# Hybrid attention and MoE layer on one core: softmax sums applied to the turned result of a head pair, attention steps in groups of two units

## What is computed

```python
h  = rms_norm(x, g_attn)
z  = h @ w_in                        # q, k, v of branch a (MoBA) and b (DSA), indexer, two gates
# branch a: causal attention; branch b: attention over the 128 keys that the indexer picks
s_own = einsum('bqhd,bhkd->bqhk', q_c, k_own) * scale        # causal mask, then
p_own = softmax(s_own, axis=-1)
o     = einsum('bqhk,bhkd->bqhd', p_own, v_own)              # softmax(scores) @ V per head
x = x + (sigmoid(ga) * (o_a @ w_br_a) + sigmoid(gb) * (o_b @ w_br_b)) @ w_out
x = x + hier_moe(rms_norm(x, g_ffn), ...)                    # 32 experts, two per token
x = x + sigmoid(rms_norm(x, g_ple) @ w_ple_gate) * (p @ w_ple_proj)
```

## Time and profile before

| | us |
|---|---|
| runs: 999.1, 998.84, 1000.87; median | 999.1 |
| profiled execution, whole | 998.48 |
| its span (first to last instruction) | 996.7 |
| busy in the span: TensorE | 967.7 (97%) |
| TensorE weight loads | 593.6 (60%) |
| VectorE | 380.4 (38%) |
| ScalarE | 305.9 (31%) |
| GpSimd | 134.7 (14%) |
| mean granted clock of TensorE | 0.997 |

### The profile page before, as it was taken

One profiled execution on the slowest core, in us unless ns is written; L12 is line 12 of the kernel. 1 busy time (PEld: TensorE's weight loads), 2 busy tenths in 40 slices (PEclk: granted clock), 3 DMA queues, 4 the chain that ended last, 5 costly groups with the idle time before them and its releaser, 6 DMA issues.

```text
span 996.7 us, 12099 instructions
## 1 busy us (share of the span) xinstructions
PE 967.7 (97%) x4818; PEld 593.6 (60%) x4818; DVE 380.4 (38%) x785; ACT 305.9 (31%) x536; POOL 134.7 (14%) x137
## 2 busy tenths in 40 slices
PE   8999999999999999999999999999998998999996
PEld 6776887676788888886434444444443443443475
DVE  4344896655353536327211111110111111013776
ACT  6445335746433214242111111111111111211555
POOL 0320234926500000000000100000000000001000
PEclk9999999999999999999999999999999999999998
DMA  9512230000082350856999999999999999999902
GB/s 333 183 49 79 85 92 2 2 1 2 1 296 85 94 195 7 350 201 249 414 391 423 419 421 421 422 421 420 421 420 420 421 420 422 415 421 405 369 1 85
DMA packets 59145, 256.05 MB, mean 257 GB/s; under 512 B 12222, under 2 KB 12862, under 8 KB 34000
## 3 DMA queue, kind: packets, MB, share of 16 engines
q1 hardware_dynamic: 50224, 248.26, 62.4%
q0 software_dynamic: 2560, 4.20, 1.1%
q10 hardware_dynamic: 6304, 2.80, 1.1%
HBM read 248.95 MB, written 10.49 MB: 260 GB/s over the span
## 4 chain that ended last, share of the span: by engine, by line
PE 81%; DMA 12%; DVE 2%; POOL 2%; ACT 2%; issue 0%; DVEq 0%; SPq 0%
PE psum L749 37%; PE psum L1119 17%; DMA slot<-in_w_up 12%; PE psum L1075 5%; PE psum L1139 4%; PE psum L1140 4%; PE psum L1095 1%; PE psum L1159 1%; PE psum L1261 1%; PE psum L1085 1%; PE psum L964 1%; PE psum L949 1%; PE psum L937 1%; POOL raw L2211 1%; PE psum L737 1%; PE psum L925 1%
## 5 line engine op out<-in xcount | busy, mean ns | idle before, releaser
L1119 PE MATMUL psum<-slot,xt 128*64 128x512 f32 x512 | 232.7, 598 | 10.1 <-DMA slot<-in_w_up 9.4
L1120 PE MATMUL psum<-slot,xt 128*64 128x512 f32 x512 | 232.9, 598 | 0.0
L1119 PEld LDWEIGHTS psum<-slot,xt 128*64 128x64 f32 x512 | 65.8, 137 | 131.9 <-issue 127.7
L1139 PE MATMUL psum<-slot,ht 128*64 128x512 f32 x256 | 115.9, 595 | 0.0
L1140 PE MATMUL psum<-slot,ht 128*64 128x512 f32 x256 | 115.9, 596 | 0.0
L749 PE MATMUL psum<-w_hi,act_hi 128*128 128x512 f32 x288 | 114.8, 399 | 0.3 <-DVE act_lo L1655 0.3
L2227 POOL DMA_INDIRECT pair_rows<-y,slot_pair x30 | 30.3, 1012 | 618.3 <-ACT y L1500 618.3
L749 PE MATMUL psum<-w_lo,act_hi 128*128 128x512 f32 x288 | 112.5, 391 | 0.0
L749 PE MATMUL psum<-w_hi,act_lo 128*128 128x512 f32 x288 | 112.3, 390 | 0.0
L574 DVE TENSOR_TENSOR w_lo<-raw,w_hi 128x2048 fp32r<-128x2048 f32 (+1 forms) x30 | 69.3, 2308 | 90.3 <-ACT w_hi L569 90.2
L1493 ACT ACTIVATE small<-psum,slot_inv 64x512 f32<-64x512 f32 x32 | 21.9, 684 | 250.3 <-PE psum L1120 249.3
(11 more groups left out here) (294 smaller groups left out, 1490.1 us busy)
## 6 DMA issues: line engine op xcount, KB each, us to landing
slot<-in_w_gate SPq DMA_DIRECT2D x64, 1024.0 KB, 21.2
slot<-in_w_up SPq DMA_DIRECT2D x64, 1024.0 KB, 20.7
slot<-in_w_down SPq DMA_DIRECT2D x64, 1024.0 KB, 22.0
raw<-in_w_in SPq DMA_DIRECT2D x21, 1024.0 KB, 5.1
raw<-in_w_out SPq DMA_DIRECT2D x4, 1024.0 KB, 5.7
pair_in<-pair_rows SPq DMA_DIRECT2D x4, 1024.0 KB, 14.8
slot<-in_w_ple_gate SPq DMA_DIRECT2D x4, 1024.0 KB, 12.3
rows_tok<-in_x SPq DMA_DIRECT2D x8, 256.0 KB, 5.2
```

The lines of the kernel that those rows point to most:

```text
L1119: mm_g = pe.matmul(ps[FIRST:2 * FIRST, :], left, g[:, k, :], start=first, stop=last)
L1120: mm_u = pe.matmul(ps[0:FIRST, :], left, u[:, k, :], start=first, stop=last)
L1139: pe.matmul(ps[0:FIRST, :], left, w[:, k, 0:512], start=first, stop=last)
```

## The change

Four things change together:

- P is no longer scaled. Its turn on TensorE waits for ScalarE's exponential (`exps_to` counts them in their new order) instead of GpSimd's scaling.
- GpSimd spreads the two inverted sums of a unit over 64 columns each (`spread_sums`) into `sums_wide`. A new step `turn_s` per head pair transposes these four blocks on TensorE into bank 5. ScalarE copies the bank into `ot_sum`, which also gives the bank back. VectorE multiplies the pair's result bank by it into `ot_sum`. GpSimd then makes the high and the low part (`split_rows`), in place of ScalarE and VectorE.
- The attention steps go in groups: scores of two units, turn of one, pv of two, turn of the next, and behind every second group `turn_s`. VectorE inverts sums for two units at a time, and ScalarE waits for the spread four units back before it writes a sum.
- The tail uses the semaphore `rooted` in place of `tail_rms`, without another change.

```diff
--- before.py
+++ after.py
@@ -101,19 +101,18 @@
 
 def attention_steps(branch, between=()):
 
-    out, between = [], list(between)
-    for u in range(LAG, NU + LAG + 1):
-        if u < NU:
-            out.append(("scores", branch, u))
-        if u < NU + LAG:
-            out.append(("turn_p", branch, u - LAG))
-        if u > LAG:
-            out.append(("pv", branch, u - LAG - 1))
-        if u >= NU - 1:
-            out += between[:2]
-            between = between[2:]
-    assert not between
-    return out
+    step = lambda kind, *units: [(kind, branch, u) for u in units]
+    pairs = [list(between[n:n + 2]) for n in range(0, 8, 2)]
+    out = []
+    out += step("turn_p", 0) + step("scores", LAG) + step("turn_p", 1) + step("scores", LAG + 1)
+    for u in range(LAG + 2, NU, 2):
+        out += step("scores", *range(u, min(u + 2, NU))) + step("turn_p", u - LAG)
+        out += step("pv", *[v for v in (u - LAG - 2, u - LAG - 1) if v >= 0]) + step("turn_p", u - LAG + 1)
+        if u > LAG + 2 and (u - LAG) % NT == 0:
+            out += step("turn_s", (u - LAG) // NT - 1)
+    out += pairs[0] + step("pv", NU - 4) + step("turn_p", NU - 2) + pairs[1] + step("pv", NU - 3)
+    out += step("turn_p", NU - 1) + pairs[2] + step("pv", NU - 2) + pairs[3] + step("pv", NU - 1)
+    return out + step("turn_s", NH // 2 - 1)
 
 def front_steps():
 
@@ -164,7 +163,7 @@
     turns = rels = outs = 0
     for s in FRONT:
         kind = s[0]
-        if kind in ("rope", "topk", "select", "merge"):
+        if kind in ("rope", "topk", "select", "merge", "turn_s"):
             continue
         if kind in WEIGHTS:
             if s[2] == 0 and s[1] != "ix":
@@ -220,7 +219,7 @@
              3: [("turn", "ix", 0)]}
 
 BESIDE_GATE = {0: [("turn_p", "b", NU - 2), ("pv", "b", NU - 3)], 1: [("turn_p", "b", NU - 1), ("pv", "b", NU - 2)],
-               2: [("pv", "b", NU - 1)], 3: []}
+               2: [("pv", "b", NU - 1), ("turn_s", "b", NH // 2 - 1)], 3: []}
 
 VB = [HALF_OF["z", "vb", i] for i in range(2)]
 
@@ -357,6 +356,7 @@
     kt_ = sb("kt", "qk", [P, NT, S], skip=8 * K)[:]
     v_sb = sb("v", "v", [P, NT, AW])[:]
     rope_t = sb("rope_t", "rope", [P, NT, NH, 2 * ROT])
+    sums_wide = sb("sums_wide", "rope", [P, 2, NT, P])
     work = sb("work", "work", [P, 9 * P])
     iqt = sb("iqt", "o", [P, NT, S], skip=8 * K)[:]
     ikt = sb("ikt", "ik", [P, S])
@@ -369,6 +369,7 @@
     ot_at = {"a": "o", "b": "stage"}
     ot_hi = {x_: sb(f"ot_{x_}_hi", ot_at[x_], [P, NT, S], F32R)[:] for x_ in "ab"}
     ot_lo = {x_: sb(f"ot_{x_}_lo", ot_at[x_], [P, NT, S], F32R, skip=8 * K)[:] for x_ in "ab"}
+    ot_sum = {x_: sb(f"ot_{x_}_sum", ot_at[x_], [P, NT, S], skip=8 * K)[:] for x_ in "ab"}
     merged = sb("merged", "qk", [P, KD, S])[:]
     inv_row = sb("inv_row", "work", [P, S])[:]
     inv_wide = sb("inv_wide", "work", [P, NT, P], skip=2 * K)[:]
@@ -475,9 +476,9 @@
     x1_hi_done, x1_low, first_picked, x1_back, tail_added = (sem(n) for n in (
         "x1_hi_done", "x1_low", "first_picked", "x1_back", "tail_added"))
     picked, x_gathered, x_copied, halves_made = sem("picked"), sem("x_gathered"), sem("x_copied"), sem("halves_made")
-    (tail_turned, tail_high, tail_ready, tail_filled, tail_gated, tail_squared, tail_rms, tail_inv, added, last_squared,
+    (tail_turned, tail_high, tail_ready, tail_filled, tail_gated, tail_squared, tail_inv, added, last_squared,
      last_ms, last_rms, last_out) = (sem(n) for n in (
-         "tail_turned", "tail_high", "tail_ready", "tail_filled", "tail_gated", "tail_squared", "tail_rms", "tail_inv",
+         "tail_turned", "tail_high", "tail_ready", "tail_filled", "tail_gated", "tail_squared", "tail_inv",
          "added", "last_squared", "last_ms", "last_rms", "last_out"))
     slot_loaded = [sem(f"slot_loaded_{k}") for k in range(SLOTS)]
     half_used = sem("half_used")
@@ -497,7 +498,8 @@
     roped, pool_chain, dve_chain = sem("roped"), sem("pool_chain"), sem("dve_chain")
     acc_done = sem("acc_done")
     max_done, mark_done = sem("max_done"), sem("mark_done")
-    exp_done, sum_inverted, p_scaled = sem("exp_done"), sem("sum_inverted"), sem("p_scaled")
+    exp_done, sum_inverted, sums_spread = sem("exp_done"), sem("sum_inverted"), sem("sums_spread")
+    sums_turned, ot_low = sem("sums_turned"), sem("ot_low")
     x_back = sem("x_back")
     ngmax_done, gexp_done, e2_done = sem("ngmax_done"), sem("gexp_done"), sem("e2_done")
     top_done, rank_done, count_done, list_done = sem("top_done"), sem("rank_done"), sem("count_done"), sem("list_done")
@@ -590,6 +592,14 @@
             eng.wait_ge(sem_, value)
 
     BR = {"a": 0, "b": 1}
+
+    def exps_to(u, h):
+
+        if LAG <= u % NU < LAG + 2:
+            return 2 * u + 2
+        if LAG + 2 <= u % NU < NU - 1:
+            return 2 * u + 2 * h + u % 2
+        return 2 * u + h + 1
 
     def turned_banks(eng, u, wait):
 
@@ -760,6 +770,8 @@
                 b = BANK[tile_of(s, t)][0]
                 if s[2] == 0:
                     claim(pe, tile_of(s, t))
+                if (s, t) == (("z", "vb", 0), 1):
+                    pe.wait_ge(sums_turned, NH)
                 if (s, t) == (("z", "qa", 0), NT - 1):
                     pe.wait_ge(ix_t, 2)
                 for k in range(k_n):
@@ -942,13 +954,23 @@
                 turned_banks(pe, s, claim)
                 if t == 2:
                     drained(pe, ("turn_p", a, i - 2, 1))
+                    if i > NT:
+                        pe.wait_ge(sums_turned, 2 * (NH // 2 * BR[a] + i // NT))
                 for h in range(2):
-                    pe.wait_ge(p_scaled, 2 * u + h + 1)
+                    pe.wait_ge(exp_done, exps_to(u, h))
                     for j in range(t + 1):
                         at = (h * (t + 1) + j) * P
                         mm = pe.transpose(bank[4 + at // S][:, at % S:at % S + P], prob[u % len(prob)][:, h, j * P:(j + 1) * P], ident)
                     if h or t == NT - 1:
                         mm.then_inc(bank_filled[BANK[s + (h if t == NT - 1 else 0,)][0]], 1)
+            elif kind == "turn_s":
+                n = NH // 2 * BR[a] + i
+                pe.wait_ge(sums_spread, NT * (n + 1))
+                if i < NH // 2 - 1:
+                    drained(pe, ("turn_p", a, NT * (i + 1), 1))
+                for t in range(NT):
+                    mm = pe.transpose(bank[5][:, t * P:(t + 1) * P], sums_wide[:, n % 2, t, :], ident)
+                mm.then_inc(sums_turned, 1)
             elif kind == "pv":
                 (pair, t), u = unit(i), NU * BR[a] + i
                 if i == 0:
@@ -977,8 +999,8 @@
             elif kind in ("branch_a", "branch_b"):
                 x_ = kind[-1]
                 if a == 0:
-                    for pair in range(NH // 2):
-                        drained(pe, ("ot", x_, pair))
+                    pe.wait_ge(ot_low, NH // 2 * (BR[x_] + 1))
+                    pe.wait_ge(sums_turned, 2 * NH)
                 half_product_turned(s, (ot_hi[x_], ot_lo[x_]), 0)
             elif kind == "out":
                 if a == 0:
@@ -1327,6 +1349,8 @@
 
             u, w = NU * BR[s[1]] + s[2], (unit(s[2])[1] + 1) * P
             n = u % len(prob)
+            if u >= len(prob):
+                act.wait_ge(sums_spread, u - len(prob) + 1)
             drained(act, s + (h,))
             act.activation(prob[n][:, h, 0:w], prob[n][:, h, 0:w], ACT.Exp, bias=nm[:, n, h:h + 1], scale=-1.0,
                            accum_out=rs[:, n, h:h + 1]).then_inc(exp_done, 1)
@@ -1401,10 +1425,9 @@
                     act.copy(prob_t[u % len(prob_t)][:, 0:w], ps[:, 0:w]).then_inc(bank_drained[BANK[s + (0,)][0]], 1)
                 if i + LAG < NU:
                     exponent(("scores", a, i + LAG), 1)
-            elif kind == "pv":
-                if i % NT == NT - 1:
-                    pair = unit(i)[0]
-                    act.copy(ot_hi[a][:, pair, :], filled(act, ("ot", a, pair))).then_inc(turn_hi, 1)
+            elif kind == "turn_s":
+                act.wait_ge(sums_turned, 2 * (NH // 2 * BR[a] + i) + 1)
+                act.copy(ot_sum[a][:, i, :], bank[5]).then_inc(sums_turned, 1)
         act.dma_start(g_in[:], g_attn[0].rearrange("(k p) -> p k", p=P), allow_slow_non_contiguous=True).then_inc(gain_in, 16)
         act.wait_ge(eps_set, 1)
         act.activation(spare[:], eps[:, 0:1], ACT.Copy, scale=eps[:, 0:1])
@@ -1573,7 +1596,7 @@
 
         def tail_roots(t):
             act.wait_ge(tail_squared, t + 2)
-            act.activation(stat[:, 4 + t:6 + t], stat[:, t:t + 2], ACT.Sqrt, scale=1.0 / D, bias=eps[:, 0:1]).then_inc(tail_rms, 1)
+            act.activation(stat[:, 4 + t:6 + t], stat[:, t:t + 2], ACT.Sqrt, scale=1.0 / D, bias=eps[:, 0:1]).then_inc(rooted, 1)
 
         gate_split_high(0)
         gate_split_high(1)
@@ -1704,7 +1727,10 @@
                     dve.tensor_tensor_reduce(out=prob[n][:, h, 0:w], in0=ps[:, 0:w], in1=bias, scale=-HD ** -0.5,
```

(45 more changed lines are left out.)

## The result

The changed kernel takes 1005.4 us (median of 5 runs, 1004.27 to 1005.45) against 999.1 us before: a ratio of 1.0056, 95% interval 1.0042 to 1.0071. It is slower by 6.3 us in the medians, 0.6%, and the interval leaves out 1. The profiled execution took 1005.4 us with a span of 1003.6 us, 6.9 us more than the span before.

What follows compares the result with a forecast made beforehand. It took attention, with TensorE nearly always busy, as what counts. Per branch 1.4 (start) + 0.85 (two pairs) + 1.8 (end) = 4.05, for two 8.1 us; 998.5 + 8.1 = 1006.6 us, range 1001 to 1010.5.

Steps and rivals of the forecast that it cites:

- the experts' loads pass a shift on: Expert weight loads start after attention's front, so a microsecond won or lost in attention moves the end by a microsecond.
- TensorE's own work: Head pair in attention: TensorE's work after the change is 8.45 us, 0.1 of it a wait, 0.8 below today's 9.27.
- the fixed part of a group: TensorE steps: each change of kind costs some 0.15 us for turns and PV, 0.21 for scores; grouping saves 0.72 a pair.
- The steady wait: Steady pairs: the 256-column turn waits 1.1 us for VectorE's copy, queued behind the multiplication; two pairs cost +0.85 a branch.
- The old wait: Steady pairs: the 0.52 us wait before the 384-column turn, ended by ScalarE's copy, goes.
- The start: Start of a branch: waits at turn 1, scores 6 and turn 3 put scores 7 at 10.5 instead of 9.09, +1.4 us.
- The end: End of a branch: PV 10 behind scores 15, a 0.1 us wait and the last two sums' turns, +1.8 us.
- off the path either way: GpSimd's new spreads, copy and subtraction take 5.5 to 6.7 us a pair, less than 9.27, so they cost nothing.
- Rival (1): Faster: the steady wait and the start's waits don't arise, -1.45 us a branch, 995.6 us; chance 0.07.
- Rival (3): Much slower: GpSimd's split holds up VectorE's scores and copies up to 3 us a pair, 1007 to 1025; chance 0.06.
- GpSimd's scaling: Attention: scaling of P leaves GpSimd; it was hidden except for short waits, so nothing was booked for it.

Runs made afterwards that it cites:

- e4: Changed kernel with the edits of e1 and e2, and the turned sums written to the next pair's result bank instead of bank 5: 996.96 us, ratio 0.9978.
- e1: Changed kernel with VectorE's multiplication of pairs 0 to 2 moved behind its copy of the next 384-column turn: 1002.45 us, ratio 1.0028.
- e2: Changed kernel with the old interleaving for units 3 to 6 of each branch, groups of two only from unit 7: 1001.0 us, ratio 1.0019.
- e9: As e4, but only the sums of pairs 0 and 1 go to the next pair's result bank, the others to bank 5: 996.08 us, ratio 0.9968.
- e8: Changed kernel with e2's edit, but P scaled by GpSimd and the result split as before the change, no sums' turn: 1000.66 us, ratio 1.0019.
- e3: Changed kernel with the edits of e1 and e2 together: 997.91 us, ratio 0.9982.

## Why the prediction was right

The sign, the mechanism of the main loss and the places were those of the working: the forecast was +8.1 us on the profiled execution, and it came to +6.9. One step of it failed without moving the sum, the wait ahead of the 384-column turn, and the 1.2 us too much come from terms a little too long: in attention a 0.07 us in the start, 0.35 in the two pairs and 0.3 in the end.

- That the experts' loads pass a shift on: right, 6.7 us at the gate and 6.7 at the first load of the chain that ended last.
- TensorE's own work and the fixed part of a group: right. Scores 7 and 8 together take 1.49 us (178.61 to 180.10), PV 2 and 3 1.25. In e4's second pair, where TensorE waits for nothing, it takes 8.29 us; I had 8.45 with 0.1 for a wait that isn't there. (The turns of the earlier trace rows add up to 2.86, where I had 2.88.)
- The steady wait: the step was right and 0.26 too long. I had the multiplication at 5.97 behind scores 7, it started at 5.82; the copy of the 384-column turn at 8.11, it started at 7.93; a wait of 1.14, it was 0.88. The sum was too long where turns of 512 columns took 1.02 us instead of 1.12 (in the pair of the earlier trace rows GpSimd scaled the second half until 187.85, 0.48 us into that turn; now nothing is scaled), and so the sums were through 0.14 sooner. Two pairs cost +0.5 instead of +0.85 a branch. e1 confirms the cause.
- The old wait: "the wait of 0.52 goes" was wrong. The working left 0.2 us ahead of the 384-column turn (5.76 to 5.96); it was 0.42, and e1 shows it again. It did not show in the pair's length, since the 256-column turn hangs on VectorE either way, but it is what e4 got back. Nor was 0.52 the wait of every pair before, as the row of 178.96 shows.
- The start: 10.42 for 10.5. Its three waits stand in the rows as walked: 171.56, 174.55, 178.02. e2 confirms the cause.
- The end: +1.5 for +1.8 a branch. Turn 13 and the sums beside it took 0.71 us in all (0.27 and 0.44), 0.36 + 0.43 in my sum, the last sums 0.41 for 0.59, and the wait of 0.1 was not there. In branch b 1.1 us of it stand ahead of the gate's first product and 0.37 beside the gate.
- GpSimd: the copy of 512 columns took 0.62 us where I had up to 1.56, the subtraction 1.27 for 1.5, the spreads 0.30 for 0.6. It was off the path either way, as said. The profile does name GpSimd's spread as what ended 0.32 us of idle time of ScalarE at 186.24, but by the count in the code the exponential there waits for a spread that was done at 180.8; what came last was VectorE's scores 10.
- Rival (1) asked for 5.2 us or less for the sums' copy; it ended 5.8 us behind the start of scores 7 (183.83 + 0.57). Its 995.6 us is close to e9's 996.1, but e9 got there by edits that the rival did not suppose, and with other parts: -0.80, -1.88 and +1.52 us in attention a for its -1.6, -1.65 and +1.8. The closeness is in part luck. Rival (3) found no support in any run: VectorE's durations stood still beside the split. (Not every VectorE step of the loop reads PSUM, as the working has it: the reciprocals read `rs` in SBUF, one input each.)

What stays open about the idea: I booked GpSimd's scaling as hidden, with nothing gained by taking it away. In the old order that holds but for a wait of 0.33 us in each branch, the row at 178.96 in attention a. In groups of two TensorE waited for it for 2.3 us in attention a of e8, but how much of the 2.8 us between e8 and e3 is the scaling and how much the place in VectorE's queue, no run separates.

## What to carry to other kernels

An instruction that keeps its size and only stands elsewhere in an in-order queue can cost time on another engine: here VectorE's 0.69 us multiplication cost TensorE 0.88 us a pair by its place. Before moving one, list what is queued behind it on its engine and who waits for each of these, and where two engines pass a buffer back and forth, put the consumer behind the work that others wait for. An order in groups that pays in the steady state needs its own start and end: here the order of four units at a branch's start decided over 4.4 us (e2), and one bank at the end of branch b over 0.9 (e9). And compare halves of a change only with the same queue order in both: e8 looks 2.8 us worse than e3 and is level with e2.

## What the runs showed of the hardware

GpSimd took 1.56 us for a tensor-scalar of 128 x 512 with a per-partition scalar, but 0.62 us for a copy to fp32r and 1.27 us for a tensor-tensor of the same size (after, 186.16 and 186.86): the operation with one tensor and a scalar per partition was the slowest of the three. The Trainium skill, page GPSIMD Engine Reference, section "3.1 Elementwise — side-by-side cycle accounting", gives about 2.6 cycles an element for the two-input form, and reckons at 1.2 GHz; by it an estimate for 512 elements is 1.1 us. The measured 1.27 us is 0.16 above that estimate; the trace does not show what the rest is.

The change of kind on TensorE costs time even where no one waits. From start to start, scores of 256 and 512 columns by themselves take 0.64 and 1.06 us, but 1.49 in a row (178.61 to 180.10), 0.21 less. PV of 12 and 8 instructions take 0.81 and 0.59 by themselves, but 1.25 in a row (181.12 to 182.37), 0.15 less. The two transposes of a 128-column turn and the four of the sums take 0.80 together in a row (182.37 to 183.17), as the six of a 384-column turn do (192.47 to 193.27 in the earlier trace rows). Why the weight loader does not run ahead there, no run settles.
